# A two-layer transformer block with an expert layer: U runs 26 steps ahead of V, the residual is parked in DRAM, and the gate stage works in two half buffers with chunks of four tokens

## The chip, the cores and the metric

The kernel runs on one core of one Trainium2 chip. The metric is the device time of one execution, in microseconds (us); less is better.

## The reference

512 tokens of width 1024 go through two blocks, in float32. The first adds 16 meta tokens and does grouped-query and differential attention and a gated FFN. The second does latent attention and forgetting attention, and then the PEER expert layer, which this change is about:

```python
qp = (h @ w_pq).reshape(b, s, PEER_HEADS, 2, PEER_HALF)        # 8 heads, 2 halves of 128
sc = jnp.einsum("bshpd,hpnd->bshpn", qp, sub_keys)             # 128 keys in each half
s1, i1 = lax.top_k(sc[..., 0, :], 16);  s2, i2 = lax.top_k(sc[..., 1, :], 16)
cand = (s1[..., :, None] + s2[..., None, :]).reshape(b, s, 8, 256)
top_s, top_c = lax.top_k(cand, 16)
expert = e1 * 128 + e2                                         # e1, e2: the keys that top_c names
gate = jax.nn.softmax(top_s, axis=-1)
y = sum over heads and selected experts of  gate * gelu(u_expert . h) * v_expert
x = x + gate2 * y
```

There are 16384 experts (128 first keys times 128 second keys), each with a row of 1024 in `peer_u` and one in `peer_v`.

## The kernel before

Everything up to the second attention and its output projection (`mixed_linear`) is not touched. The rest has five stages.

**Key scores.** TensorE (`pe`) projects the queries and multiplies them with the keys, 16 pieces; ScalarE (`act`) evacuates them into `sc` (part of the SBUF arena `r2`).

**Sort.** VectorE (`v`) does `key_tops` and `pair_tops` for each of 8 heads and the first three of four token tiles (`DT` = 3, 384 tokens, `DN`); 24 pairs. `top_done` counts them.

**Picks.** `tile_picks(t)` finds, for each tile, the keys of the 128 chosen experts of a token: `pair_ranks`, a one-hot over 16 ranks (`hot`, 2048 elements a partition, L1470), a multiply (L1473) and a reduction (L1475), twice, then the softmax sums. TensorE turns the result around (`slot_transposes`) and ScalarE evacuates it to `slotT`.

**Gates.** For the three tiles the chosen experts are not gathered; all 16384 are computed, and a dense matrix of gates (token by expert) says what counts. For every token it is the product of two one-hot matrices: VectorE writes `one1` for a chunk of eight tokens in one operation (L1531) and `one2` in eight (L1535, one a token, which multiplies the gate in); TensorE does one 128x128 matmul a token (L2056); ScalarE copies 4 tokens at a time from PSUM to `stage` (L901), one buffer for a whole tile, 8 MB. SyncE (`sp`) stores the tile to the DRAM tensor `gd` in four pieces of 2 MB (`store_gates`, L439), and ScalarE may write the next tile only when they have landed (`stage_free`). Two chunk buffers stand in a ring.

**Expert loop.** Step i takes the 128 experts with second key i. The U part (`experts_in`): load 512 KB of `peer_u`, transpose it (`u_transposes`, two halves), split it into a high part (ScalarE, `u_high`, L845) and a rest (VectorE, `u_low`, L1488), three matmuls for each of eight pieces against the split tokens (`hidden`, L2007), and a gelu (ScalarE) into a slot of `act_ring`. The V part (`experts_out`, L2023): multiply the ring slot with the gates (`w_mul`), split that and 512 KB of `peer_v`, and 18 matmuls of 512 columns, which add up in six PSUM banks over all 128 steps. The gates come back 768 KB at a time for four steps (`load_gates`, L447). U runs `AHEAD` = 16 steps ahead of V: two such steps lie before the chunks, twelve among them (one after every fourth chunk), two after, and the loop does the other 112 along with V; its last 16 steps have V alone. The first `u_transposes` stands in TensorE's queue behind all key scores, and VectorE's first `u_low` behind all sorting.

The fourth tile's 128 tokens are done otherwise: GpSimd (`pool`) gathers single rows of U and V by indirect DMA (512 KB for 128 tokens), VectorE does one dot or one multiply-add for each of the 2 x 128, spread evenly over the steps from `FIRST_ROW` = 4 to `LAST_ROW` = 112, and sorts this tile's heads there too.

The residual `x` (2 MB) stays in SBUF to the end, where VectorE adds the expert sums and SyncE stores the result.

Each engine works its queue off in the order of the code and waits on semaphores; SyncE's queue holds all loads and stores of this part in one written-out order.

Of the kernel before, what the change touches and what calls it, by code (L numbers as in the profile page):

```python
# [15 lines left out]
P = 128  # L16
D = 1024
# [21 lines left out]
AHEAD = 16  # L39
CHUNK = 8  # L40
# [3 lines left out]
FIRST_ROW, LAST_ROW = 4, 112  # L44
# [29 lines left out]
def build(nc, wst, wada, x_in, meta_in, cols_in, rowsa_in, rowsb_in, rope_in, const_in, pos_in,  # L74
          subk_in, peer_u, peer_v, out):
    ctx = ExitStack()
    with ctx:
# [149 lines left out]
        keys = cut(r1, 10752, NKEYS)  # L227
# [7 lines left out]
        act_ring = cut(r2, 0, AHEAD, DN)  # L235
# [10 lines left out]
        stage = cut(big, 0, NKEYS, P)  # L246
        one1 = cut(r1, 0, 2, CHUNK, P)
        one2 = cut(r1, 2 * CHUNK * P, 2, CHUNK, P)
        slotT = [gates[:, 0, 0:384], gates[:, 0, 384:768], r1[:, 10240:10624]]
        hot = cut(big, 0, SLOTS, TOPK)  # L250
        ranks = cut(big, 2048, 2, SLOTS)
        rank_bits = cut(big, 2304, 2, SLOTS).bitcast(U32)
        topf = cut(big, 2560, 2, PH, TOPK)
        wrap = cut(big, 2816, SLOTS)
        picks = cut(big, 2944, DT, 2, SLOTS)

        gring = cut(big, 0, 2, DT, GB * P)
# [21 lines left out]
        gd = nc.dram_tensor("gd", (DT, P, NKEYS * P), F32).ap()  # L279
# [42 lines left out]
        one1_ready, one2_ready, g_acc, g_ev = (sem(n) for n in ("one1_ready", "one2_ready", "g_acc", "g_ev"))  # L322
        g_out = [sem(f"g_out{q}") for q in range(4)]
# [11 lines left out]
        y_ready, y_out = sem("y_ready"), sem("y_out")  # L335
# [64 lines left out]
        def stage_free(eng, t):  # L400

            if t:
                for q in range(4):
                    eng.wait_ge(g_out[q], 16 * t)
# [5 lines left out]
        def _(sp):  # L410
# [25 lines left out]
            def store_gates(t):  # L436
                sp.wait_ge(g_ev, 2 * NCH * (t + 1))
                for q in range(4):
                    sp.dma_start(gd[t][:, 4096 * q:4096 * q + 4096], stage[:, 32 * q:32 * q + 32, :].rearrange("p e t -> p (e t)")  # L439
                                 ).then_inc(g_out[q], 16)  # L440

            def load_gates(b):
                if b % 8 == 0:
                    sp.wait_ge(g_out[b // 8], 16 * DT)
                if b >= 2:
                    sp.wait_ge(w_done, GB * (b - 1))
                sp.dma_start(gring[:, b % 2],  # L447
                             gd[:, :, GB * P * b:GB * P * b + GB * P].rearrange("t p n -> p t n")).then_inc(g_in[b % 2], 16)
# [5 lines left out]
            for j in range(9, 12):  # L454
                load_u(j)
            store_gates(1)
            for j in range(12, 16):
                load_u(j)
            store_gates(2)
            sp.wait_ge(g_acc, 2 * DT * NCH)  # L460
            for i in range(VR):
                load_v(i)
            for b in range(2):
                load_gates(b)
            for j in range(AHEAD, AHEAD + 2):
                load_u(j)
            for i in range(NE):
                if i + AHEAD + 2 < NE:
                    load_u(i + AHEAD + 2)
# [5 lines left out]
            sp.dma_start(out[DT], x[:, DT, :]).then_inc(y_out, 16)  # L475
            for t in range(DT):
                sp.wait_ge(y_ready, t + 2)
                sp.dma_start(out[t], x[:, t, :]).then_inc(y_out, 16)
# [4 lines left out]
        def _(pool):  # L483
# [44 lines left out]

            for q in range(2, 4):
                pool.wait_ge(g_out[q], 16 * DT)  # L530
# [11 lines left out]
        def _(act):  # L542
# [298 lines left out]
            def u_high(s):  # L841
# [3 lines left out]
                act.activation(uT_hi[:, s % 2], ps[:, 1, :].rearrange("p (k n) -> p k n", k=KD // 2), ACT.Copy  # L845
# [14 lines left out]
            def gelu(j):  # L860
# [3 lines left out]
                act.activation(act_ring[:, j % AHEAD, :], ps[:, 0, 0:DN], ACT.Gelu_apprx_tanh,  # L864
# [14 lines left out]
            def slots_evac(t):  # L879
                act.wait_ge(slot_tr, t + 1)  # L880
                act.activation(slotT[t], ps[:, 2 + t % 2, 0:384], ACT.Copy).then_inc(slot_ready, 1)

            for s in range(3):
# [1271 lines left out]
```

## Time and profile before

| | |
|---|---|
| median of 3 runs | 2830.1 us (2827.2 to 2830.22) |
| the profiled execution: its time, its span | 2838.91 us, 2837.1 us |
| TensorE matmul busy | 2532.2 us (89%) |
| VectorE busy | 1786.5 us (63%) |
| ScalarE busy | 955.8 us (34%) |
| GpSimd busy | 355.3 us (13%) |
| mean granted TensorE clock | 0.955 |
| moved by DMA | 427.20 MB, mean 151 GB/s |

Times in rows are counted from the start of the span. "Busy" is a share of the whole span, over stages that have different limits, so the stages are read one by one below. The granted clock is a share of 2.4 GHz. PE is TensorE, PEld its weight loads, DVE VectorE, ACT ScalarE, POOL GpSimd, SP SyncE; a q behind a name is the engine's queue. In the program's names `r` stands for the arenas `r1` and `r2`.

### The profile page before, as it was taken

Reading aid. Unit: us, or ns where it says so; the run is one execution under the profiler, and the core shown is the slowest. Engines: PE = TensorE matmul, PEld = TensorE weight load, DVE = VectorE, ACT = ScalarE, POOL = GpSimd, SP = SyncE. Lnnn points to the kernel's source line nnn. Section 1 sums busy time; section 2 is a strip of 40 time slices with the busy share of each in tenths; the row PEclk is TensorE's granted clock in tenths of the full one; section 3 lists DMA queues with packets and bytes.
Section 4 is the critical chain, followed back from the end, with each engine's and each line's share of the span. In section 5 each row is a group of like instructions: output and inputs, shape, how many; then the busy total and the mean of one; then the engine's idle time right before and its main releaser. Section 6 shows DMA issues by size and latency. Waiting matters only on the chain.

```text
span 2837.1 us, 37492 instructions
## 1 busy us (share of the span) xinstructions
PE 2532.2 (89%) x13633; PEld 2153.2 (76%) x13633; DVE 1786.5 (63%) x3871; ACT 955.8 (34%) x1639; POOL 355.3 (13%) x326
## 2 busy tenths in 40 slices
PE   8999888999989969989256669999999999999998
PEld 6777776777779747854156668898989898899986
DVE  5535646553244455458887657877777777776675
ACT  3334412222224446311134444333333333333332
POOL 1001100110000000100000001232222222222220
PEclk9999989999999989999678899999999999999999
DMA  4110005662222110030003345787777777777764
GB/s 172 61 45 1 1 33 183 228 216 88 79 86 75 60 45 1 1 126 1 8 23 141 149 170 190 261 292 261 268 261 270 265 269 267 266 272 277 244 224 141
DMA packets 107908, 427.20 MB, mean 151 GB/s; under 512 B 11328, under 2 KB 11584, under 8 KB 97104
## 3 DMA queue, kind: packets, MB, share of 16 engines
q1 hardware_dynamic: 62624, 262.17, 26.2%
q0 software_dynamic: 44064, 160.98, 16.3%
q8 instruction: 111, 1.82, 0.3%
q10 hardware_dynamic: 1040, 1.67, 0.2%
q14 instruction: 69, 0.57, 0.1%
HBM read 397.51 MB, written 27.26 MB: 150 GB/s over the span
## 4 chain that ended last, share of the span: by engine, by line
PE 73%; DVE 14%; issue 4%; ACT 4%; DMA 2%; DVEq 2%; ACTq 1%; SPq 1%; POOLq 0%
PE ps L2023 16%; PE ps L2007 15%; PE ps L1808 9%; PE ps L1762 7%; PE ps L1678 5%; PE ps L1830 4%; PE ps L1996 3%; PE ps L2056 3%; PE ps L1743 2%; DMA gd<-big 1%; PE ps L1948 1%; PE ps L1715 1%; PE ps L1929 1%; ACT r L639 1%; PE ps L1730 1%
## 5 line engine op out<-in xcount | busy, mean ns | idle before, releaser
L2007 PE MATMUL ps<-hd_hi,uT_hi 128*128 128x384 f32 x1024 | 349.4, 341 | 0.7 <-ACT r L864 0.7
L2007 PE MATMUL ps<-hd_hi,uT_lo 128*128 128x384 f32 x1024 | 347.4, 339 | 0.0
L2007 PE MATMUL ps<-hd_lo,uT_hi 128*128 128x384 f32 x1024 | 347.3, 339 | 0.0
L1488 DVE TENSOR_TENSOR uT_lo<-ps,uT_hi 128x512 fp32r<-128x512 f32 x256 | 176.7, 690 | 255.0 <-ACT uT_hi L845 254.8
L2023 PE MATMUL ps<-v_hi,ew_hi 128*128 128x512 f32 x768 | 320.4, 417 | 3.9 <-DVE v_lo L1493 2.1
L2023 PE MATMUL ps<-v_hi,ew_lo 128*128 128x512 f32 x768 | 303.1, 395 | 0.0
L2023 PE MATMUL ps<-v_lo,ew_hi 128*128 128x512 f32 x768 | 300.9, 392 | 0.0
L537 POOL DMA_INDIRECT big<-peer_u,r x128 | 136.0, 1062 | 861.6 <-DVE r L1563 524.8
L845 ACT ACTIVATE uT_hi<-ps 128x512 fp32r<-128x512 f32 x256 | 152.9, 597 | 266.3 <-PE ps L1996 266.3
L864 ACT ACTIVATE r<-ps,zero 128x384 f32<-128x384 f32 x128 | 74.3, 581 | 472.0 <-PE ps L2007 467.7
L1996 PE MATMUL ps<-const,r 128*128 128x128 f32 x1024 | 155.3, 274 | 52.5 <-DVE uT_lo L1488 32.9
L2007 PEld LDWEIGHTS ps<-hd_hi,uT_hi 128*128 128x128 f32 x1024 | 193.6, 189 | 10.0 <-issue 1.1
L2007 PEld LDWEIGHTS ps<-hd_hi,uT_lo 128*128 128x128 f32 x1024 | 193.3, 189 | 9.7
L2007 PEld LDWEIGHTS ps<-hd_lo,uT_hi 128*128 128x128 f32 x1024 | 193.3, 189 | 0.0
L537 POOL DMA_INDIRECT big<-peer_v,r x128 | 144.4, 1128 | 386.2 <-DVE big L1591 369.8
L1493 DVE TENSOR_TENSOR v_lo<-r,v_hi 128x1024 fp32r<-128x1024 f32 x128 | 156.8, 1225 | 34.3 <-ACT v_hi L852 34.3
L1996 PEld LDWEIGHTS ps<-const,r 128*128 128x128 f32 x1024 | 126.4, 141 | 65.6 <-DVE uT_lo L1488 25.5
L1591 DVE SCALAR_TENSOR_TENSOR big<-big,r 128x1024 f32<-128x1024 f32 x128 | 164.5, 1285 | 16.6 <-DMA big<-peer_v,r 4.3
L2023 PEld LDWEIGHTS ps<-v_hi,ew_lo 128*128 128x128 f32 x768 | 144.2, 188 | 32.6
L2023 PEld LDWEIGHTS ps<-v_hi,ew_hi 128*128 128x128 f32 x768 | 144.7, 188 | 27.9 <-DVE v_lo L1493 4.6
L2023 PEld LDWEIGHTS ps<-v_lo,ew_hi 128*128 128x128 f32 x768 | 145.2, 189 | 24.3
L1073 DVE TENSOR_TENSOR w_lo<-big,w_hi 128x2048 fp32r<-128x2048 f32 x42 | 96.2, 2290 | 106.1 <-ACT w_hi L632 106.1
(332 smaller groups left out, 5335.2 us busy)
## 6 DMA issues: line engine op xcount, KB each, us to landing
big<-wst SPq DMA_DIRECT2D x70, 1024.0 KB, 4.8
r<-peer_u SPq DMA_DIRECT2D x128, 512.0 KB, 7.2
r<-peer_v SPq DMA_DIRECT2D x128, 512.0 KB, 5.2
r<-wada POOLq DMA_DIRECT2D x48, 512.0 KB, 4.7
gd<-big SPq DMA_DIRECT2D x12, 2048.0 KB, 15.1
big<-gd SPq DMA_DIRECT2D x32, 768.0 KB, 9.4
x<-x_in SPq DMA_DIRECT2D x4, 512.0 KB, 6.7
big<-peer_u,r POOLq DMA_INDIRECT x128, 6.4
```

What stands on the lines that cost most here:

```text
L537: pool.indirect_dma_start(rows[n % RW], None, table, bass.IndirectOffsetOnAxis(ap=idx[:, n:n + 1], axis=0)).then_inc(got[n % RW], 16)
L845: act.activation(uT_hi[:, s % 2], ps[:, 1, :].rearrange("p (k n) -> p k n", k=KD // 2), ACT.Copy).then_inc(u_hi_done, 1)
L1488: v.tensor_tensor(uT_lo[:, s % 2], ps[:, 1, :].rearrange("p (k n) -> p k n", k=KD // 2), uT_hi[:, s % 2].bitcast(F32), ALU.subtract).then_ ...
L1493: v.tensor_tensor(v_lo[:, i % VR, :], vraw[:, i % VR, :], v_hi[:, i % 2, :].bitcast(F32), ALU.subtract).then_inc(v_lo_done, 1)
L1591: v.scalar_tensor_tensor(out=yacc[:, n % 2, :], in0=vrows[n % RW], scalar=wts[:, n:n + 1], in1=yacc[:, n % 2, :], op0=ALU.mult, op1=ALU.ad ...
L1678: mm = pe.matmul(ps[0:r, bank, 0:w], hT[:, k, t * P:t * P + r], wt[:, k, 0:w], start=(k == 0), stop=(k == KD - 1))
L1762: mm = pe.matmul(ps[:, bank, 0:256], h[:, k, t * P:(t + 1) * P], w[:, k, :], start=(k == 0 and i == 0), stop=(k == KD - 1 and i == 2))
L1808: mm = pe.matmul(ps[:, 2 * (f % 2) + u, :], w[:, k, u, :], h[:, k, 0:512], start=(k == 0 and i == 0), stop=(k == KD - 1 and i == 2))
L1830: mm = pe.matmul(ps[:, 2 * t + half, :], a[:, f % 2, t * P:(t + 1) * P], w[:, f % 2, 512 * half:512 * half + 512], start=(f == 0 and i == ...
L1996: mm = pe.transpose(ps[:, 1, P * k:P * k + P], uraw[:, j % UR, at:at + P], ident)
L2007: mm = pe.matmul(ps[:, 0, 0:DN], w[:, k, :], h[:, KD // 2 * half + k, :], start=(half == 0 and k == 0 and i == 0), stop=(half == 1 and k = ...
L2023: mm = pe.matmul(ps[:, 2 + 2 * t + half, :], w[:, P * t:P * t + P], vv[:, 512 * half:512 * half + 512], start=(i == 0 and n == 0), stop=(i ...
```

## The change

It does the following.

- `AHEAD` is 26. Nine U steps (0 to 8) are put into the sort and just behind it: from the 17th of the 24 sorts on, VectorE does two `u_low` behind each sort (`hidden_low`), a ninth pair comes after the ranks of tile 0. Steps 9 and 10 follow, twelve come among the chunks (one after every eighth chunk of four), three after the chunks. The loop has 102 U steps, and 26 with V alone.
- Until U is 26 ahead, its transposes use two PSUM banks in turn (`in_bank`), not one.
- The 26 slots of `act_ring` need room: ten lie in the SBUF of `x`. So `x` is stored to a DRAM tensor `xd` before (ScalarE's first `u_high` waits for that), and loaded back into `xback` at step 106, for the end. `LAST_ROW` is 102: the 256 row operations are spread over 98 steps. The last sum of the fourth tile comes at step 112, as before.
- The gates are built in chunks of four tokens, in a ring of four buffers (`one`); one PSUM bank holds a chunk. `stage` is two buffers of half a tile (64 tokens, 4 MB) each. ScalarE issues their stores itself, four of 1 MB, behind the last copy of the half. `gd` has six halves, so a load of gates for four steps has runs of 1 KB, not 2 KB.
- The picks: the one-hots of both keys stand in one buffer. `tile_ranks(t)` writes them, and the multiply is done by GpSimd (`slot_keys`; for tile 0 VectorE does one of the two). `tile_picks(t)` waits for that and does one reduction for both keys. Tile 0 is picked before the chunks; tiles 1 and 2 are picked by VectorE in the middle of the chunks of the tile before (ranks after its third chunk, the rest after its seventh).
- SyncE asks for the U load 26 ahead of the gate loads and keeps three U loads ahead, not two.

```diff
-AHEAD = 16
-CHUNK = 8
+AHEAD = 26
+INX = 10
+FIRST = 11
+EVERY = 8
+HT = P // 2
+CHUNK = 4
-FIRST_ROW, LAST_ROW = 4, 112
+FIRST_ROW, LAST_ROW = 4, NE - AHEAD
...
+        def in_bank(s):
+
+            return 3 if s % 2 and s < 2 * AHEAD else 1
...
             sp.wait_ge(mixt_tr, 2 * T)
-            for j in range(9):
+            for j in range(UR):
                 load_u(j)
-            store_gates(0)
...
+            sp.wait_ge(out_add, 8 * T)
+            for t in range(T):
+                sp.dma_start(xd[t], x[:, t, :]).then_inc(x_out, 16)
+            for j in range(UR, AHEAD):
                 load_u(j)
...
+            load_u(AHEAD)
             for b in range(2):
                 load_gates(b)
...
+                if i == LAST_ROW + 4:
+                    sp.wait_ge(u_row, SLOTS)
+                    sp.wait_ge(v_row, SLOTS)
+                    sp.wait_ge(x_out, 16 * T)
+                    for t in range(T):
+                        sp.dma_start(xback[t], xd[t]).then_inc(x_back, 16)
...
+            def slot_keys(t):
+                pool.wait_ge(ranks_ready, t + 1)
+                for a in range(2 if t else 1):
+                    hk = hot[:, a].rearrange("p (h k) r -> p h k r", h=PH)
+                    mk = pool.tensor_tensor(hk, hk, each_pick(a), ALU.mult)
+                mk.then_inc(hot_ready, 1)
...
+            def hidden_evac(j):
+                u_high(2 * j + 1)
+                u_high(2 * j + 2)
+                gelu(j)
...
+                    if at + CHUNK == HT:
+                        act.wait_ge(g_ev, n + 1)
+                        for q in range(4):
+                            act.dma_start(gd[h][:, 32 * HT * q:32 * HT * q + 32 * HT],
+                                          stage[h % 2][:, 32 * q:32 * q + 32, :].rearrange("p e t -> p (e t)")).then_inc(g_out[h % 2][q], 16)
+                    if n % EVERY == EVERY - 1:
+                        hidden_evac(FIRST + n // EVERY)
...
+            def hidden_low(steps):
+                for j in steps:
+                    u_low(2 * j + 1)
+                    u_low(2 * j + 2)
...
                     pair_tops(t, h).then_inc(top_done, 1)
+                    u = DT * h + t - 16
+                    if u == 0:
+                        u_low(0)
+                    if u >= 0:
+                        hidden_low([u])
+            tile_ranks(0)
+            hidden_low([8])
...
+            tile_picks(0)
+            hidden_low([9])
             for t in range(DT):
                 v.wait_ge(slot_ready, t + 1)
                 for c in range(NCH):
                     n = t * NCH + c
+                    if n == 3:
+                        hidden_low([10])
+                    if n >= 4:
+                        v.wait_ge(g_acc, n - 3)
+                    v.tensor_tensor(one[n % 4][0], each(keys, CHUNK), over(slotT[t][:, CHUNK * c:CHUNK * c + CHUNK], NKEYS),
+                                    ALU.is_equal)
...
+                    if t < DT - 1 and c == 2:
+                        tile_ranks(t + 1)
+                    if t < DT - 1 and c == 6:
+                        tile_picks(t + 1)
```

## Rows read from the trace of the kernel before

**Rows 1.** Busy by stage: span, PE, PEld, DVE, ACT, POOL, PEclk, DMA share, GB/s:

```profile
1360.00:1450.00 90.00, 16.25 (x78) 14.65 (x76) 74.01 (x177) 8.59 (x14) 0.00 (x0) 0.58 0.04 12
...
1449.30:1516.10 66.80, 52.95 (x380) 49.84 (x379) 59.16 (x161) 37.60 (x44) 0.00 (x0) 0.97 0.10 30
1516.10:1537.00 20.90, 5.60 (x43) 5.25 (x41) 10.25 (x28) 0.90 (x2) 0.00 (x0) 0.72 0.96 408
...
1912.90:2755.00 842.10, 836.33 (x4513) 758.32 (x4512) 628.73 (x997) 289.76 (x471) 229.40 (x209) 1.00 0.76 264
2768.10:2826.20 58.10, 58.09 (x251) 47.28 (x252) 30.33 (x39) 19.18 (x26) 0.00 (x0) 1.00 0.44 141
```

**Rows 2.** Chain that ended last, one loop step apart (start, length):

```profile
2679.22 2.77 PE ps L2023 x12
...
2688.47 2.77 PE ps L2023 x12
```

**Rows 3.** Timeline of TensorE, the first transposes of U:

```profile
1359.86 0.60 PE L1996 MATMUL ps<-const,r 128*128 128x128 f32 x4
1385.76 1.11 PE L1996 MATMUL ps<-const,r 128*128 128x128 f32 x4 [25.30 <-DVE uT_lo L1488]
```

**Rows 4.** Timeline of VectorE, end of the sort and a tile's picks:

```profile
1379.31 0.22 DVE L1450 TENSOR_SCALAR r<-r 128x16 f32<-128x16 f32 x1
...
1384.70 0.22 DVE L1450 TENSOR_SCALAR r<-r 128x16 f32<-128x16 f32 x1
...
1391.56 0.28 DVE L1467 CAST big<-r 128x256 f32<-128x256 uint32 x1
...
1393.36 2.29 DVE L1470 TENSOR_TENSOR big<-big,const 128x2048 f32<-128x2048 f32 x1
...
1408.59 0.29 DVE L1467 CAST big<-r 128x256 f32<-128x256 uint32 x1
```

**Rows 5.** VectorE in the gate stage: timeline, then lines (min/median/max, first to last):

```profile
1484.84 1.22 DVE L1531 TENSOR_TENSOR r<-r,gates 128x1024 f32<-128x1024 f32 x1
1485.97 2.14 DVE L1535 TENSOR_SCALAR r<-r,gates 128x128 f32<-128x128 f32 x8
1488.03 1.22 DVE L1531 TENSOR_TENSOR r<-r,gates 128x1024 f32<-128x1024 f32 x1
...
1498.20 0.69 DVE L1488 TENSOR_TENSOR uT_lo<-ps,uT_hi 128x512 fp32r<-128x512 f32 x1 [0.54 <-ACT uT_hi L845]
...
L1531 DVE TENSOR_TENSOR r<-r,gates x32: 1210/1215/1226, 1449.3 to 1586.9; 128x1024 f32<-128x1024 f32 x32
...
L1535 DVE TENSOR_SCALAR r<-r x128: 335/342/348, 1591.2 to 1670.6; 128x128 f32<-128x128 f32 x128
```

**Rows 6.** Waits from 1300 to 1740 (total, times, longest):

```profile
ACT big L901 <- DMA gd<-big: 37.3, 2, 18.7
```

**Rows 7.** Timelines of SyncE and TensorE at the hand-over:

```profile
1674.23 3.07 SPq L439 DMA_DIRECT2D gd<-big  x4
...
1681.24 5.32 SPq L447 DMA_DIRECT2D big<-gd  x2
...
1706.62 1.12 PE L1996 MATMUL ps<-const,r 128*128 128x128 f32 x4 [19.61 <-DMA r<-peer_u]
...
1712.94 0.47 PE L2023 MATMUL ps<-v_hi,ew_hi 128*128 128x512 f32 x1 [1.80 <-DVE ew_lo L1508]
```

**Rows 8.** A load issued by ScalarE (timeline), and SyncE's gate stores (their line):

```profile
2.15 0.62 ACTq L546 DMA_DIRECT2D r<-rope_in x1
...
L439 SPq DMA_DIRECT2D gd<-big x12: 326/671/1371, 1513.9 to 1676.0; - x12
```

**Rows 9.** VectorE's combining line in attention, and GpSimd beside it (timeline):

```profile
L1101 DVE SCALAR_TENSOR_TENSOR r<-r,coef x16: 767/768/2993, 205.1 to 359.6; 128x528 f32<-128x528 f32 x16
...
341.38 2.62 DVE L1101 SCALAR_TENSOR_TENSOR r<-r,coef 128x528 f32<-128x528 f32 x1
...
338.90 4.53 POOL L492 TENSOR_TENSOR w_lo<-big,w_hi 128x2048 fp32r<-128x2048 f32 x1
```

More of the change, by code:

```diff
@@ L244, in build @@
         gst = cut(r2, 16960, 2, T * PH)
-        stage = cut(big, 0, NKEYS, P)
-        one1 = cut(r1, 0, 2, CHUNK, P)
-        one2 = cut(r1, 2 * CHUNK * P, 2, CHUNK, P)
+        stage = [cut(big, NKEYS * HT * b, NKEYS, HT) for b in range(2)]
+        one = [[cut(r1, CHUNK * P * (2 * b + a), CHUNK, P) for a in range(2)] for b in range(4)]
         slotT = [gates[:, 0, 0:384], gates[:, 0, 384:768], r1[:, 10240:10624]]
[L250 to L257, printed above, removed]
+        xback = [cut(big, 8192 + D * i, D) for i in range(T)]
+        hot = cut(r2, 0, 2, SLOTS, TOPK)
+        rank_bits = cut(r2, 14368, 2, SLOTS).bitcast(U32)
+        ranks = cut(r2, 14624, 2, SLOTS)
+        wrap = cut(big, NKEYS * P, SLOTS)
+        topf = cut(r1, 11104, 2, SLOTS)
+        picks = [v.rearrange("p (a s) -> p a s", a=2) for v in (gates[:, 0, 768:1024], r1[:, 10848:11104], rowsb[:, 0:256])]
+        gring = cut(big, 0, 2, 2 * DT, GB * HT)
         w_of = cut(big, 4096, 2, DN)
@@ L434, in load_v @@
                 sp.dma_start(vraw[:, i % VR, :], v_by_key[:, i, :]).then_inc(v_load[i % VR], 16)
[L436 to L440, printed above, removed]
             def load_gates(b):
                 if b % 8 == 0:
-                    sp.wait_ge(g_out[b // 8], 16 * DT)
+                    gates_out(sp, b // 8)
                 if b >= 2:
@@ L908, in _ @@
-            for j in range(2 + 4 * DT, AHEAD):
-                u_high(2 * j + 1)
-                u_high(2 * j + 2)
+            act.wait_ge(x_out, 16 * T)
+            u_high(0)
+            for j in range(9):
+                hidden_evac(j)
+                if j in (5, 6, 7):
+                    gate_exps(j - 5)
+            slots_evac(0)
+            for j in range(9, FIRST):
+                hidden_evac(j)
+            for t in range(DT):
+                for c in range(NCH):
+                    n = t * NCH + c
+                    h, at = n * CHUNK // HT, n * CHUNK % HT
+                    if at == 0:
+                        stage_free(act, h)
+                    act.wait_ge(g_acc, n + 1)
+                    act.activation(stage[h % 2][:, :, at:at + CHUNK].rearrange("p e t -> p t e"),
+                                   ps[:, 4 + n % 4, :].rearrange("p (t e) -> p t e", t=CHUNK), ACT.Copy).then_inc(g_ev, 1)
+                    if t < DT - 1 and c == 16:
+                        slots_evac(t + 1)
+                    if at + CHUNK == HT:
[5 more added lines that the diff above has]
+                        hidden_evac(FIRST + n // EVERY)
@@ L911, in _ @@
+            for j in range(FIRST + DT * NCH // EVERY, AHEAD):
                 if j < AHEAD - 1:
-                    gelu(j)
+                    hidden_evac(j)
+                else:
+                    u_high(2 * j + 1)
+                    u_high(2 * j + 2)
             w_high(0)
@@ L1483, in tile_picks @@
                 v.tensor_tensor(g, g, over(gst[:, 1, PH * t:PH * t + PH], TOPK), ALU.mult)
+                if t == 0:
+                    hk = hot[:, 1].rearrange("p (h k) r -> p h k r", h=PH)
+                    v.tensor_tensor(hk, hk, each_pick(1), ALU.mult)
+                    v.drain()
+                v.wait_ge(hot_ready, t + 1)
+                v.tensor_reduce(picks[t], hot, AX.X, ALU.add)
                 v.drain().then_inc(picks_ready, 1)
@@ L2041, in _ @@
             u_transposes(0)
-            experts_in(0)
-            for t in range(DT):
-                slot_transposes(t)
-            experts_in(1)
+            for j in range(9):
+                experts_in(j)
+            slot_transposes(0)
+            for j in range(9, FIRST):
+                experts_in(j)
             for t in range(DT):
```

181 lines of the change are left out of this document (81 added, 100 removed).

## The prediction

> **What bounds the kernel now.** I read the page's slices first. The reader is to see that PE is full in the last 40% of the span and has its one deep hole just before it; so the question is what fills the hole and what the last part costs per step. Then the stages [rows 1]: in the expert loop (1912.9 to 2755) PE is busy 836.3 of 842.1 us, DVE 75%, DMA 76% at 264 GB/s. That loop is bound by TensorE. One of its steps is 9.25 us [rows 2]. The last steps, without U, are 252 matmuls (14 steps of 18) in 58.1 us [rows 1], 4.15 us each. So a U step (8 transposes, 24 matmuls) costs 9.25 - 4.15 = 5.10 us of PE wherever PE is full, and nothing where PE is idle. From 1360 to 1450 PE is busy 16.3 of 90 us at a granted clock of 0.58, a mean over its two levels of 1.2 and 2.4 GHz [rows 1]: VectorE is sorting and picking.
>
> Next the hole itself. PE does its first U transposes at 1359.86 and then waits 25.3 us for VectorE's first split of U [rows 3]. VectorE sorts until 1384.9, one (tile, head) every 5.39 us, then makes three tiles' picks at 17.03 us each (1391.56 to 1408.59) [rows 4], ending at 1442.6. Of a tile's 17.03 the ranks take 1.8 (to 1393.36), the gate sums about 1.0, and six operations over 2048 elements the rest, 2.37 each with their gaps (2.29 without). In the gate stage VectorE writes a chunk of eight tokens in 3.19 us (1.13 the first one-hot, 2.06 the eight others) and serves one U step per four chunks [rows 5]; the chunk stage is VectorE's, except for two stalls in which ScalarE waits 37.3 us for the single stage buffer to be stored [rows 6]. Last, the hand-over: the last store is issued at 1674.2, the gates are asked for at 1681.2, PE waits 19.6 us for a U load that queued behind all that, and the first V matmul starts at 1712.94 [rows 7].
>
> **Part 1, ten U steps leave the loop.** 112 U steps become 102: 10 x 5.10 = **-51.0 us**, if PE stays the bound. What gets tighter is VectorE: the 256 row operations are now spread over 98 steps and not 108, 2.61 a step for 2.37, so 0.24 x 1.3 us = 0.3 us more in 9.25, from 75% to about 79%. DMA gains 0.24 x 0.5 MB a step, 13 GB/s on 264. Both stay below PE, but heads' sorting steps fall more often on steps with three rows; I charge **+3 us** (bounds 0 and +12).
>
> **Part 2, the sort stage gets nine U steps.** The first split can't come before PE's transposes at 1359.9 and ScalarE's copy, 1361.1. VectorE is through with its seventeenth sort at 1346.9 (1384.7 [rows 4] less seven of 5.39, with the last operation of 0.2) and so stands still for 14 us. This is the cost that the edit hides: the PE queue, where the U work stands behind all key scores. Then u_low 0, 1 and, after one `hidden` (2.1 us) and its transposes, u_low 2: about 1366.2. The other seven sorts now carry two splits each, 5.39 + 2 x 0.65 = 6.7 us (PE needs 5.1 per step, so it keeps up): 1366.2 + 47 = 1413. The picks of tile 0: ranks 1.8 us, two one-hots of 2.37, so 1419.6; two splits, the keys, the gate sums (1.0), one multiply 2.37, a reduction over twice the elements (2 x 2.29 less one overhead, 4.45). With the lock of part 3 this ends at 1431.4. The splits 19 and 20 then wait for PE (slot transposes, one `hidden`), as they did before (6.7 us from 1442.6 to 1449.3); with two banks I take 5.7. Chunks start at **1437**, and did at 1449.3 [rows 5].
>
> **Part 3, the gate stage.** A chunk of four is one one-hot of 128x512 (0.69, the length of u_low [rows 5], less 0.08 overlap = 0.61) and four of 0.2575: 1.64 us; 96 make 157.4. Twelve pairs of splits, 1.3 each: 15.6. The stage buffer is halved and doubled; a half takes over 30 us to fill, a store of 4 MB at 408 GB/s [rows 1] takes 10: the 37.3 us of waiting vanish. Two tiles' picks moved in here: ranks and one-hots 6.5, gates and reduction 5.5: 24.0. The store issues are now on ScalarE: its issues take up to 0.62 us, SyncE's 0.67 in the median [rows 8]. Four, 2 us or more, stand ahead of u_high; the evacuation of the last chunk before it leaves about 0.9 us of slack there, so VectorE waits about 1 us at five halves: +5 (bounds 0 and 12).
> What remains is GpSimd's multiply, 4.53 us for 128x2048 [rows 9]. VectorE's own was 2.37. Is it free, being beside VectorE? The trace speaks against it. A VectorE operation with two SBUF inputs has a median of 768 ns, but 2.62 us where it starts at 341.38 beside a GpSimd multiply that ends at 343.43: it ends 0.57 us after that one. The longest, 2993 ns, lies the same way [rows 9]. So VectorE's two-input work stood still until GpSimd was done. The one-hots have two SBUF inputs; I charge the whole of the four multiplies of tiles 1 and 2, 4 x 4.53 = 18 us, and tile 0 about 2 (in part 2). Bounds: 0 and 22.
> The Trainium skill (SBUF — State Buffer, "Who interferes with whom") says the same: the port pair is locked for a whole instruction by VectorE with two SBUF inputs or in a two-port mode, or by GpSimd, and the other blocks. By it the sum is as here; a reader who takes engines as independent gets 20 us less.
> Sum: 157.4 + 15.6 + 24.0 + 18 + 5 = 220. The last one-hot ends at **1657** (before 1670.9 [rows 5]).
>
> **Part 4, the hand-over.** PE has four U steps left, about 5.2 each: 1657.6 + 21 = 1678.5, then 2 us until the weights are there (1.8 before). The data: from 1659 on 4 MB of gates, 1.5 of V, 0.5 of U, 1.5 of gates back, 7.5 MB at 400 GB/s = 19 us: 1678. The U load no longer stands behind the gate loads. V starts at about **1681**, 32 us before 1712.9. If the small runs of the gate loads (1 KB for 2 KB) land late, this grows by some 5 us; none of this stage is at full rate otherwise.
>
> **Part 5, the residual.** Four stores of 0.5 MB queue on SyncE behind three U loads, which started at 1260; nothing needs them before 1359.9, so 95 us hide about 5. The reload (2 MB) comes at step 106, in the stage that moves 141 GB/s at a DMA share of 0.44 [rows 1]; V loads queue behind it, a step later. 0 to 1 us. The end (11 us of sums and stores after the last matmul at 2826) is as it was.
>
> **Sum** against the profiled execution (span 2837.1, 2838.9 with what lies around): -32 - 51 + 3 = -80, so 2759. The median of the runs is 8.8 us below that execution: **2750**.
>
> **Rivals.**
> A: the two engines do not hinder each other in these forms (the trace has no one-hot beside a GpSimd operation). Then 20 us less, 2730. For it: nothing but that it hasn't been seen.
> B: VectorE is not kept fed in the gate stage: ScalarE's stores, its copies in strides, and the order split, gelu, evacuation in one queue hold up `u_hi_done`, say 1.5 us more at each of 24 splits; 24 x 1.5 = 36, of which GpSimd's blocks already cover some, so about +20 us: 2770. Against: ScalarE has only 37.6 of 66.8 us busy in the stage now [rows 1].
> C: the loop gives back. If the denser rows let VectorE's lateness through, 0.3 us in each of 98 steps, +29: 2778. Against: PE idle in the loop is 5.8 us in all [rows 1].
> D, slower than before: the loads bind the loop. Each step moves 2.5 MB, with denser rows 2.62, and the gates come in runs half as long. It takes 80 us to eat the gain, 0.8 us in each of 102 steps: a step of 10.05 us, a rate of 261 GB/s. The loop sustains 264 now at a share of 0.76 [rows 1], so this needs a fall of the rate itself.
> E: no change: ten U steps saved but the front loses all it wins and 50 more; the PE idle there is too large for that.
>
> **How the numbers follow.** Likeliest as summed 0.45; A 0.18; B 0.19; C 0.13; D 0.03; E 0.02. The range 2722 to 2784 leaves out about 2 in 10 (half of the far ends of A and C, D, E). Measurement tells 0.2%, 6 us, from no change: faster 0.95, same 0.02, slower 0.03.
>
> **What would show it.** In the changed trace: VectorE idle about 14 us before its first split near 1347; sorts at 6.7 us after; chunks from 1437 at 1.64 us, and one-hots of several us wherever GpSimd multiplies (right) or of their usual length (A); no wait of ScalarE for a gate store; last one-hot at 1657; first V matmul at 1681; a loop step of still 9.25 us, 26 last steps of 4.15. The prediction is wrong if the loop step is longer, or if the first V matmul comes after 1700.

## The result: 2793.6 us, 1.4% faster, half of what was forecast

| | before | after |
|---|---|---|
| median, lowest to highest (4 runs each) | 2830.16 us, 2827.2 to 2832.83 | 2793.55 us, 2787.02 to 2798.95 |
| ratio to before, 95% interval | 1 | 0.9859 (0.9841 to 0.9876) |
| the profiled execution: time, span | 2838.91, 2837.1 us | 2790.66, 2788.9 us |
| mean granted TensorE clock | 0.955 | 0.965 |

The forecast was 2750 us with a range of 2722 to 2784. The sign was right, the size was not: 36.6 us came, 80 had been worked out. The page of the kernel after: busy time by engine, then the slices of PE, its granted clock and the DMA share; the last line is PE's in the kernel before.

```profile
PE 2545.9 (91%) x13633; PEld 2162.6 (78%) x13633; DVE 1795.6 (64%) x3911; ACT 965.7 (35%) x1644; POOL 390.0 (14%) x331
...
PE   8999888999989969989857789999999999999998
...
PEclk9999989999999979999989899999999999999999
DMA  4110005662221210021113246787878778787764
...
PE   8999888999989969989256669999999999999998
```

The hole in front of the expert loop is smaller: its lowest slice is 5 tenths, not 2. GpSimd has 390.0 us for 355.3, the five multiplies among them. The stages, as in [rows 1]; first the sort and tile 0's picks, then the gate stage, the hand-over, a piece of the loop and the last steps without U:

```profile
1360.00:1437.00 77.00, 56.14 (x307) 51.19 (x305) 66.56 (x230) 25.11 (x38) 4.50 (x1) 0.93 0.20 69
1437.00:1670.00 233.00, 169.57 (x1134) 161.56 (x1135) 204.34 (x513) 112.72 (x131) 18.89 (x4) 0.88 0.30 116
1670.00:1698.20 28.20, 22.45 (x138) 21.07 (x137) 7.59 (x11) 9.70 (x17) 0.00 (x0) 1.00 0.94 345
1910.00:2640.00 730.00, 719.08 (x3849) 651.14 (x3848) 562.45 (x900) 251.20 (x408) 226.00 (x198) 0.99 0.79 274
2700.00:2777.80 77.80, 75.56 (x323) 61.23 (x322) 42.83 (x54) 25.19 (x34) 0.00 (x0) 0.98 0.46 146
```

Two things differ from what was expected. In the gate stage VectorE is busy only 204.34 of 233 us, although its work sets that stage's length. In the loop PE is idle 10.9 of 730 us and the mean clock is 0.99; before it was 5.8 of 842 at 1.00 [rows 1].

From here on the path is cut at four points that each trace shows: the first one-hot of the chunks, the start of the last one, the first V weight load, and the last V weight load. In front of them stands the last weight load of the query projection (3 us before the last key score; "last query" in the table), up to which only SyncE's part is changed: the stores of `x`. It comes at 1355.5 us in the profile before and at 1347.5 after, at 1344.9 to 1352.1 in the experiments on the changed kernel: profiles of the same code differ by that much. So stages are compared, not times.

| us | last query | to first one-hot | chunks | to first V matmul | V loop |
|---|---|---|---|---|---|
| before | 1355.5 | 93.8 | 221.3 | 42.3 | 1113.1 |
| after | 1347.5 | 84.0 | 237.5 | 29.1 | 1079.5 |
| e1_sync_stores | 1344.9 | 84.0 | 212.9 | 28.2 | 1074.2 |
| e2_act_stores_late | 1346.6 | 84.0 | 213.9 | 28.9 | 1076.4 |
| e3_vector_multiplies | 1348.1 | 84.0 | 233.7 | 29.0 | 1074.1 |
| e4_rows_to_112 | 1350.5 | 86.8 | 234.9 | 29.0 | 1095.9 |
| b1_rows_to_102 | 1349.0 | 94.2 | 219.3 | 42.2 | 1122.1 |
| e5_picks_in_two_steps | 1346.6 | 84.0 | 212.9 | 28.4 | 1062.9 |
| e6_sync_stores_vector_multiplies | 1352.1 | 83.1 | 210.4 | 28.5 | 1079.0 |
| e7_start_late_every_six | 1344.9 | 66.7 | 217.2 | 28.1 | 1074.1 |
| e8_all_four | 1352.0 | 64.4 | 214.5 | 28.4 | 1062.6 |

**Where it went.** The first V matmul was forecast for 1681 us and the V loop at 1113.1 - 51 + 3 = 1065 us; measured are 1698.2 and 1079.5. So the miss of 31.7 us (2790.7 against 2759) is 17.2 in front of the loop and 14.4 in it. In front: chunks began at 1431.6, not 1437 (-5.4: 8.0 earlier on account of the untouched part, 2.6 later by their own), took 237.5, not 220 (+17.5), and the hand-over took 29.1, not 24 (+5.1).

**The gate stage.** Timeline of ScalarE in the kernel after, where the first half of a tile is full:

```profile
1482.50 1.11 ACT L938 ACTIVATE big<-ps 128x512 f32<-128x512 f32 x1 [0.56 <-PE ps L2125]
1483.64 3.73 ACTq L945 DMA_DIRECT2D gd<-big  x4
1487.47 1.08 ACT L875 ACTIVATE uT_hi<-ps 128x512 fp32r<-128x512 f32 x2 [3.86 <-issue]
```

and of VectorE, which waits for that `u_high`, here and three halves later:

```profile
1488.10 0.69 DVE L1542 TENSOR_TENSOR uT_lo<-ps,uT_hi 128x512 fp32r<-128x512 f32 x1 [3.60 <-ACT uT_hi L875]
...
1610.06 0.69 DVE L1542 TENSOR_TENSOR uT_lo<-ps,uT_hi 128x512 fp32r<-128x512 f32 x1 [3.64 <-ACT uT_hi L875]
```

The four issues hold ScalarE for 3.7 us. The prediction had 2 us and 0.9 us of slack. All five halves inside the stage show it; their VectorE waits are 3.60, 3.91, 3.48, 3.64 and 3.51 us, 18.1 in all. Behind three of them comes another, of 1.1 to 2.1 us, for the chunk matmuls that now run late (5.1 in all). The waits of the whole stretch from 1400 to 1700, after; the last line is ScalarE's own:

```profile
DVE uT_lo L1542 <- ACT uT_hi L875: 45.6, 18, 5.6
...
ACT uT_hi L875 <- issue: 19.5, 5, 4.2
...
DVE r L1596 <- PE ps L2125: 5.1, 3, 2.1
```

**The lock.** GpSimd's multiplies in the kernel after (timeline), and what VectorE did beside them:

```profile
1409.38 4.50 POOL L552 TENSOR_TENSOR r<-r 128x2048 f32<-128x2048 f32 x1 [199.62 <-DVEq L1510]
1443.07 9.49 POOL L552 TENSOR_TENSOR r<-r 128x2048 f32<-128x2048 f32 x2 [29.19 <-DVEq L1510]
1530.52 9.40 POOL L552 TENSOR_TENSOR r<-r 128x2048 f32<-128x2048 f32 x2 [77.96 <-DVEq L1510]
```

```profile
1406.97 9.07 DVE L1509 TENSOR_TENSOR r<-r,const 128x2048 f32<-128x2048 f32 x2
...
1444.29 3.89 DVE L1596 TENSOR_TENSOR r<-r,gates 128x512 f32<-128x512 f32 x1
1448.10 5.32 DVE L1600 TENSOR_SCALAR r<-r,gates 128x128 f32<-128x128 f32 x4
1453.34 0.68 DVE L1596 TENSOR_TENSOR r<-r,gates 128x512 f32<-128x512 f32 x1
```

One chunk, 1.6 us a little later, takes 9.1 us here (1444.29 to 1453.4): GpSimd multiplies from 1443.07 to 1452.56. So the forecast's lock holds, in forms that the trace before did not show: the one-hot goes up to 4.42 us from 0.68, and a `tensor_scalar` with one SBUF tensor input (its two scalars come from SBUF too) to 4.55 from 0.34. Four operations in the gate stage are held up so, by 15.3 us in all. Tile 0's two one-hots take 9.07 us for 2 x 2.29: the second is held up by 4.4.

**The loop.** Timelines of VectorE and TensorE in the kernel after, at the step behind the one with the fourth tile's head picks:

```profile
1925.46 1.22 DVE L1650 CUSTOM_DVE_ANT_0 big<-big,r 128x1024 f32<-128x1024 f32 x1
...
1926.60 0.25 DVE L1621 CAST r<-r 128x16 f32<-128x16 uint32 x2
...
1931.39 0.18 DVE L1632 CAST r<-r 128x16 uint32<-128x16 f32 x1
1931.87 0.56 DVE L1557 TENSOR_TENSOR big<-big,r 128x384 f32<-128x384 f32 x1 [0.30 <-issue]
1932.34 0.68 DVE L1542 TENSOR_TENSOR uT_lo<-ps,uT_hi 128x512 fp32r<-128x512 f32 x1
```

```profile
1933.17 0.66 PE L2067 MATMUL ps<-const,r 128*128 128x128 f32 x4 [2.65 <-DVE uT_lo L1542]
...
1934.48 0.63 PE L2094 MATMUL ps<-v_hi,ew_lo 128*128 128x512 f32 x1
1934.91 0.63 PE L2094 MATMUL ps<-v_hi,ew_hi 128*128 128x512 f32 x1
...
1937.28 0.39 PE L2094 MATMUL ps<-v_hi,ew_hi 128*128 128x512 f32 x1
1937.51 0.40 PE L2094 MATMUL ps<-v_lo,ew_hi 128*128 128x512 f32 x1
```

Here VectorE has three row operations (1922.33 to 1926.6) and the picks, 5 us (1926.60 to 1931.6), in one step. `u_low` is late, PE waits 2.65 us, and then the first matmuls of V follow each other every 0.43 us where it is 0.23 otherwise: the granted clock from 1933.7 to 1937.1 is 0.51, the lower of its two levels, which costs eight matmuls 1.6 us. The step is 13.64 us long, 4.39 more than 9.25. Four steps behind picks look like this (13.64, 13.54, 13.32, 13.3), each with 3.4 us at the low clock. In the kernel before the steps behind picks are 10.4 to 11.0 us, and the clock is never low from the first V matmul to the last.

Three rows beside the picks are not enough to explain it. The kernel before has such a step too (VectorE's rows and the first operation of its picks, then TensorE's wait behind them):

```profile
2080.96 1.28 DVE L1591 SCALAR_TENSOR_TENSOR big<-big,r 128x1024 f32<-128x1024 f32 x1
...
2082.77 1.21 DVE L1581 CUSTOM_DVE_ANT_0 big<-big,r 128x1024 f32<-128x1024 f32 x1
...
2084.08 1.28 DVE L1591 SCALAR_TENSOR_TENSOR big<-big,r 128x1024 f32<-128x1024 f32 x1
2085.28 0.24 DVE L1552 CAST r<-r 128x16 f32<-128x16 uint32 x2
...
2091.49 0.63 PE L1996 MATMUL ps<-const,r 128*128 128x128 f32 x4 [1.33 <-DVE uT_lo L1488]
```

What does separate the steps is the number of rows in the three steps that a head takes (two of sorting, then the picks), as `row_step` and `head_step` of the kernel give it. From the third head on it is 7 for all six heads before, with waits of 0.96 to 1.54 us behind the picks. After it is 8 for four heads, whose waits are 2.65, 2.52, 2.52 and 2.28 us, and 7 for the other two, whose waits are 1.36 and 0.96. In the last two of a head's three steps VectorE is busy 8.1 to 8.9 of 9.25 us and hardly ever waits for `u_high` any more (0.2 us, once): what is left of a step is less than the 1.3 us of one row more.

Step by step the loop adds up. The excess over 9.25 us is 24.1 us in nine U steps after (1.5 of it in the very first, at the low clock) and 9.1 in seven before: +15.0. The steps without U have 2.4 us more. Together that is the 17.4 by which 1079.5 is over 1113.1 - 51.

### The profile page after: what moved, and what is told of

Its sections match the earlier page's. It is cut to its first block, busy times and chain, and to the rows that moved or that the text cites. A ratio compares the mean times of both kernels' runs of the same rounds, so it can differ in the third digit from the quotient of the medians.

```text
span 2788.9 us, 37588 instructions
## 1 busy us (share of the span) xinstructions
PE 2545.9 (91%) x13633; PEld 2162.6 (78%) x13633; DVE 1795.6 (64%) x3911; ACT 965.7 (35%) x1644; POOL 390.0 (14%) x331
## 4 chain that ended last, share of the span: by engine, by line
PE 73%; DVE 16%; ACT 4%; issue 3%; DVEq 2%; ACTq 1%; DMA 1%; POOL 0%
PE ps L2094 15%; PE ps L2078 14%; PE ps L1878 9%; PE ps L1832 7%; PE ps L1748 5%; PE ps L1900 4%; PE ps L2038 4%; DVE r L1600 3%; PE ps L2067 3%; DVE r L1596 2%; PE ps L1813 2%; PE ps L2018 1%; DVE uT_lo L1542 1%; PE ps L1785 1%; PE ps L1999 1%
## 5 line engine op out<-in xcount | busy, mean ns | idle before, releaser
L1542 DVE TENSOR_TENSOR uT_lo<-ps,uT_hi 128x512 fp32r<-128x512 f32 x256 | 175.7, 689 | 217.2 <-ACT uT_hi L875 216.6
L567 POOL DMA_INDIRECT big<-peer_u,r x128 | 143.0, 1117 | 487.1 <-DVE r L1650 287.3
L1650 DVE CUSTOM_DVE_ANT_0 big<-big,r 128x1024 f32<-128x1024 f32 x128 | 155.4, 1217 | 3.8 <-DMA big<-peer_u,r 3.8
L1832 PE MATMUL ps<-w_lo,h_hi 128*128 128x256 f32 x544 | 153.9, 283 | 0.0
```

The source lines that it names most:

```text
L567: pool.indirect_dma_start(rows[n % RW], None, table, bass.IndirectOffsetOnAxis(ap=idx[:, n:n + 1], axis=0)).then_inc(got[n % RW], 16)
L1542: v.tensor_tensor(uT_lo[:, s % 2], ps[:, in_bank(s), :].rearrange("p (k n) -> p k n", k=KD // 2), uT_hi[:, s % 2].bitcast(F32), ALU.subtra ...
L1650: v.tensor_tensor_reduce(out=urows[n % RW], in0=urows[n % RW], in1=h2, scale=1.0, scalar=0.0, op0=ALU.mult, op1=ALU.add, accum_out=dots[:, ...
L1832: mm = pe.matmul(ps[:, bank, 0:256], h[:, k, t * P:(t + 1) * P], w[:, k, :], start=(k == 0 and i == 0), stop=(k == KD - 1 and i == 2))
```

## The experiments

Each is the kernel after with one edit, unless said otherwise. The brackets hold the kernel before, run on the same chip.

**e1_sync_stores: who issues the gate stores.** Two theories: (1) four issues on ScalarE stand before `u_high`; (2) it is the lock, or a feed of VectorE in general.

```diff
+            store_after = {14 + 2 * h: h for h in range(2 * DT)}
             for j in range(UR, AHEAD):
                 load_u(j)
+                if j in store_after:
+                    h = store_after[j]
+                    sp.wait_ge(g_ev, HT // CHUNK * (h + 1))
+                    for q in range(4):
+                        sp.dma_start(gd[h]..., stage[h % 2]...).then_inc(g_out[h % 2][q], 16)
...
-                    if at + CHUNK == HT:
-                        act.wait_ge(g_ev, n + 1)
-                        for q in range(4):
-                            act.dma_start(gd[h]..., stage[h % 2]...).then_inc(g_out[h % 2][q], 16)
```

> The changed kernel with one part undone: the six half-stage stores are issued by SyncE again (between its U loads), not by ScalarE. Theory 1 (ScalarE's four store issues, 3.7 us in a row, stand ahead of the copy that VectorE's next split waits for; VectorE then idles 3.5 to 3.9 us and TensorE's late hidden costs 2 us more, five times): 2793 falls by 20 to 25 us, to about 2771, and the splits behind a half wait under 1 us. Rival (the waits come from the order split, gelu, evacuation in ScalarE's queue, whoever stores): no change, 2790 to 2797, and the waits of 3.5 us stay.

Measured: 2762.22 us (2757.1 to 2767.41) [2833.31], ratio 0.9755 (0.9739 to 0.9771); 31 us below the kernel after. The chunks take 212.9 for 237.5 us. Waits of e1 from 1400 to 1700, its `u_low` being L1544:

```profile
DVE uT_lo L1544 <- ACT uT_hi L882: 30.7, 18, 3.8
```

15 of 45.6 us of waiting are gone by that row, and at the halves inside the stage no such wait is left. Theory 1 holds, and in the stage its size too (20 to 25 expected): 24.6 us for five halves, 4.9 each. The waits themselves are 3.5 to 3.9; the rest, 1.3 each on average, is what comes late behind them. Some of that may be the clock: after has three stretches at the low clock, 17 us in all (from 1490, 1575 and 1609), that e1 has not. Of the other 6.7 us of the medians 5.3 are in the V loop, whose code is the same: e1 has two stretches at the low clock in it, the kernel after six. That part is not shown to belong to the stores.

**e2_act_stores_late: engine or place?** The stores stay on ScalarE, behind the two `u_high` and the gelu.

```diff
-                    if at + CHUNK == HT:
...
                     if n % EVERY == EVERY - 1:
                         hidden_evac(FIRST + n // EVERY)
+                    if at + CHUNK == HT:
...
```

> The changed kernel with ScalarE's store issues moved behind the two copies and the gelu of the U step, not ahead of them. Theory 1: the split is served first, the stores then delay only the evacuation of the next chunks, for which there are four banks: the same gain as with SyncE's stores, about 2771 (one look, so within 6 us). Rival: what is gained at the splits is lost again as waits for PSUM banks: 2790 or more.

Measured (one run): 2762.8 us; chunks 213.9, so the wait for banks that the rival expected does not come. The issues still take their time. Timeline of ScalarE in e2:

```profile
1486.68 0.58 ACT L894 ACTIVATE r<-ps,zero 128x384 f32<-128x384 f32 x1 [1.51 <-PE ps L2078]
1486.69 3.15 ACTq L947 DMA_DIRECT2D gd<-big  x4
1489.88 1.05 ACT L938 ACTIVATE big<-ps 128x512 f32<-128x512 f32 x1 [2.62 <-PE ps L2125]
```

3.15 us, with only copies of chunks behind them, for which the ring of four chunk buffers and banks is a cushion. So it is the place in the queue that costs, not the engine.

**e3_vector_multiplies: is GpSimd's multiply worth it?** The five multiplies go back to VectorE.

```diff
-            slot_keys(0)
-            for t in range(1, DT):
-                slot_keys(t)
...
-                if t == 0:
-                    hk = hot[:, 1].rearrange("p (h k) r -> p h k r", h=PH)
...
-                v.wait_ge(hot_ready, t + 1)
+                for a in range(2):
+                    hk = hot[:, a].rearrange("p (h k) r -> p h k r", h=PH)
+                    v.tensor_tensor(hk, hk, each_pick(a), ALU.mult)
```

> The changed kernel with the five 128x2048 multiplies of the picks given back to VectorE (2.29 us each there, 4.5 to 4.7 on GpSimd); everything else as changed. Theory 2 (VectorE stands still while GpSimd multiplies): gone are the blocks, 18.9 us in the gate stage and 4.4 us in the second one-hot of tile 0; added are 5 x 2.37 = 11.9 us; so 11 us faster than the changed kernel, about 2782. Rival (the engines work side by side and the long one-hots have another cause): 12 us slower, about 2805.

Measured: 2786.21 us (2781.93 to 2793.2), ratio 0.9842 (0.9824 to 0.9859); 7 us below the kernel after, whose 0.9859 (0.9841 to 0.9876) overlaps that; 11 were expected. Chunks 233.7 for 237.5. The lines of VectorE from 1430 to 1680 in e3 (busy, mean ns):

```profile
L1596 DVE TENSOR_SCALAR r<-r,gates 128x128 f32<-128x128 f32 x256 | 71.1, 342 | 0.0
L1592 DVE TENSOR_TENSOR r<-r,gates 128x512 f32<-128x512 f32 x64 | 43.9, 685 | 5.2 <-PE ps L2121 4.9
```

With no GpSimd multiply beside them the one-hots have their usual length on average, so the 4.4 us ones come from it: the longest one-hot of the chunks is 0.69 us here. **e6_sync_stores_vector_multiplies** is both edits:

> The changed kernel with SyncE's stores and with the five multiplies on VectorE. If the two costs are independent (theory 2 holds beside theory 1): 2762 less the 7 to 11 us that the multiplies gave alone: 2751 to 2755. If part of the blocks is hidden in waits that the stores left: 2758 or more.

Measured: 2758.76 us (2754.2 to 2765.99), ratio 0.9733 (0.9717 to 0.9749), against e1's 0.9755 (0.9739 to 0.9771): the intervals overlap, and 2751 to 2755 had been expected if the two costs were independent. Chunks 210.4 for 212.9. The four multiplies in the stage save VectorE 4 x 2.29 us of its own work, 9.2, and cost by the two pairs 9.2 + 2.5 to 9.2 + 3.8, about 12 to 13 us. VectorE stood still for 15.3 us; the difference comes back as waits, which within the stage rise from 2.2 us in e1 to 6.1 in e6. What the lock takes is a little more in the stage than what the hand-over to GpSimd gives, and the medians show no gain from it either way.

**e4_rows_to_112 and b1_rows_to_102: the denser rows.** e4 undoes the one line in the kernel after, b1 makes it alone in the kernel before. The line does more than its name says: the steps of the heads' sorting and picks are worked out from the rows' (`head_step`), so picks come every 12 or 13 steps, not every 13 or 14, and the fourth tile's last sum and the reload of `x` move along.

```diff
-FIRST_ROW, LAST_ROW = 4, NE - AHEAD
+FIRST_ROW, LAST_ROW = 4, 112
```

> The changed kernel with the row operations of the fourth tile spread to step 112 again (108 steps, 2.37 a step) and not to 102; the reload of the residual comes ten steps later. Theory 3 (denser rows on top of a head's sorting make VectorE late, TensorE waits and its clock drops: single steps of 13.5 us): the steps behind a head's picks fall from 13.5 to about 10.7 us, 12 to 14 us in all; but ten steps that have V alone now carry 2.4 rows each, 5.4 us of VectorE for 4.15 of TensorE, +12 us: in sum 2786 to 2796, and the step lengths tell. Rival (the 13.5 us come from the distance of 26 or from the gate loads' short runs): they stay, and the sum is 2805.

> The kernel before with one constant changed: its 256 row operations end at step 102, not 112, so 2.61 a step for 2.37; U still runs 16 steps ahead, chunks, buffers and stores as before. Theory 3 (the density of the rows at a head's picks makes the long steps, not the distance of 26): the steps behind the picks of a head rise from 10.4 to 11.0 to 12 to 13.7 us, with short drops of the clock there, so the loop grows by 10 to 18 us: 2842 to 2850. Rival (the long steps belong to the new distance, ring or gate loads): 2830 to 2834.

Measured, e4: 2810.09 us (2805.0 to 2814.82), ratio 0.9918 (0.99 to 0.9935), 17 us above the kernel after. Its steps behind the picks are 10.43 to 11.17 us, as before the change, with no low clock among its U steps but the very first: that part was right. But ten steps without U, 103 to 112, now have row operations, and they take 69.1 us for 42.5; 12 more had been expected, 26.6 came, with four stretches at the low clock, 17 us, among them. Waits of e4 from 2650 to 2790:

```profile
PEld ps L2094 <- DVE v_lo L1547: 28.1, 12, 5.3
PE ps L2094 <- DVE v_lo L1547: 22.9, 11, 4.9
```

A step of 4.15 us has no room for 2.4 rows of 1.3 us beside VectorE's own work; a step of 9.25 has. So `LAST_ROW` = 102 is the better of the two in this kernel.

Measured, b1: 2839.56 us (2832.07 to 2845.77, 10 runs) [2833.1, 13 runs], ratio 1.0021 (1.0009 to 1.0033), +6.5 us; its V loop is 9.0 longer. Steps of 11.77, 13.55, 13.28 and 13.65 us appear behind the picks, and three stretches of 3.4 us at the low clock, none of which the kernel before has. Waits of TensorE in the loop of b1 (from 1730), of the kernel after and of e5, below (from 1700); in the kernel before they are 7.6 us in 7 times, 1.5 at most:

```profile
PE ps L1996 <- DVE uT_lo L1488: 14.3, 8, 2.6
```

```profile
PE ps L2067 <- DVE uT_lo L1542: 14.8, 8, 2.6
```

```profile
PE ps L2074 <- DVE uT_lo L1544: 4.5, 7, 0.8
```

So one line, with nothing else of the change, brings the wait of 2.6 us and the low clock behind it; what it changes at the picks is the 8 rows for 7. The size was expected higher, 10 to 18.

**e5_picks_in_two_steps: thin the heaviest step.** This is e1 in which the picks of a head (from the second on) are spread over two steps, one key side in each.

```diff
-            def picks3(h):
+            def picks3(h, sides):
...
+                    elif part == 2:
+                        picks3(h, [0] if h else [0, 1])
+                    elif h:
+                        picks3(h, [1])
```

> The changed kernel with SyncE's stores (2762) and, for heads 1 to 7 of the fourth tile, the picks divided over two loop steps, one key's half in each. Theory 3 (it is the amount of VectorE work in one step, three rows and a part of a head's sorting, that makes TensorE wait and its clock drop): the seven long steps (10.3 to 13.7 us) come down towards 9.25, 8 to 14 us in all: about 2752. Rival (they have another cause, such as the loads): same as 2762, steps of 12 to 13.6 us remain.

Measured: 2746.89 us (2745.7 to 2754.2) [2832.5], ratio 0.9702 (0.9684 to 0.972), 15 us below e1 (the profiled V loop: 11.3); 8 to 14 had been expected. The V loop is 1062.9 us; PE's waits for `u_low` are down to 4.5 us, 0.8 at most, in the row above, no U step but the first (10.8, at the low clock) is over 10.3, and no other U step is at the low clock. All the work is still there; only its crowding into one step is gone.

**e7_start_late_every_six: the 14 us in which VectorE waits.** Timeline of VectorE in the kernel after, its first split:

```profile
1353.21 1.29 DVE L1542 TENSOR_TENSOR uT_lo<-ps,uT_hi 128x512 fp32r<-128x512 f32 x2 [14.35 <-ACT uT_hi L875]
```

VectorE stands still here for the key scores; so e7 is e1 with the splits beginning behind the 21st sort, five U steps in the sort stage and one among the chunks after every sixth chunk.

```diff
-FIRST = 11
-EVERY = 8
+FIRST = 7
+EVERY = 6
...
-                    u = DT * h + t - 16
+                    u = DT * h + t - 20
```

> The changed kernel with SyncE's stores and the U steps shifted: the first split stands behind the 21st sort, not the 17th, five steps (not nine) come before the picks of tile 0, and the twelve among the chunks become sixteen, one after every sixth chunk. Theory 4 (VectorE's 14.4 and 2.9 us of waiting behind the 17th sort are lost time, since TensorE's first transposes stand behind the key scores, and TensorE has room among the chunks): both waits vanish, no work is added: 15 to 17 us faster than 2762, about 2746. Rival (a group of six chunks and a U step is bound by ScalarE, six evacuations and a U step's copies and gelu, 11.7 us, or TensorE's order, not by VectorE's 11.1): half of it is lost, 2754 or more.

Measured: 2754.53 us (2743.91 to 2756.18), ratio 0.9725 (0.9709 to 0.9741), against e1's 0.9755 (0.9739 to 0.9771). By the table the way to the first one-hot is 17.3 us shorter and the chunks are 4.3 longer; from the last query to the first V matmul it is 312.0 us for 325.1, 13.1 less. 7.7 of them show in the medians. About 2746 had been expected, 2754 or more by the rival. The profiled execution, 2743.91, is e7's fastest by 9 us, so how much of the 15 is lost is not settled.

**e8_all_four: the four edits together** (stores on SyncE, multiplies on VectorE, picks in two steps, the late start).

> SyncE's stores, multiplies on VectorE, picks of a head in two steps, and the shifted U steps together. If the four mechanisms are independent: 2762 - 8 - 10 - 16, about 2728. If they cover each other (a wait removed shows the next one behind it): 2740 or more.

Measured: 2730.33 us (2726.56 to 2734.82), ratio 0.9633 (0.9617 to 0.9649), 63 us below the kernel after, near the 2728 expected if the four are independent. It is the best version found. Slices of PE and of its clock in e8:

```profile
PE   8998978999998978989868799999999999999998
...
PEclk9999989999999998999989999999999999999999
```

## Why the prediction was wrong, step by step

**Part 1, ten U steps leave the loop: the -51 us right, the +3 mis-sized.** e5, in which nothing else disturbs the loop, has 1062.9 us against 1113.1: -50.2. The +3 us, for which the bounds were 0 and 12, measured 17.4: 13.5 in the U steps behind the first, which go with the denser rows, 1.5 in the first, 2.4 in the steps without U. b1 has 11.4 in its U steps for the rows alone (and gets 2.5 back at the end of the loop, so +9.0). The prediction looked at the mean load (79% of VectorE) and at PE's idle time of 5.8 us; what counted was the heaviest stretch: a head's three steps with 8 rows, picks at the end. [Rows 1] can't show that; the steps behind the picks in the kernel before, 10.4 to 11.0 us with a PE wait of up to 1.5, could: they were already the place where VectorE is late, and the prediction looked at a regular step only [rows 2]. Rival C's mechanism is this, in four steps of about 13.5 us and not in 0.3 us everywhere. b1, e4 and e5 show the cause, too much VectorE work close together: `LAST_ROW` alone brings it, `LAST_ROW` back removes it from the U steps, picks halved remove it too. That it is the count of 8 for 7 is read from the code and the traces; no run changed the rows of one head alone. The low clock behind each such wait adds 1.6 us; the prediction had no term for it. In e1, whose loop has the same code, two of the four steps are without it and are 11.98 and 11.75 us long for 13.3. The regular step is 9.25 us as forecast, so the sign "a longer loop step" would have pointed to these four alone.

**Part 2, the sort stage: right.** VectorE waits 14.35 us (14 forecast). Behind it the sort with its splits ends at 1405.2, 57.7 us after the last query; 1413 was forecast, 57.5 after its own. Tile 0's picks took 26.4, not 24: the second one-hot was held up by GpSimd's multiply, 4.4 us where "about 2" were charged. That is the 2.6 us by which the chunks began late.

**Part 3, the gate stage: the store term failed.** The step "VectorE waits about 1 us at five halves: +5 (bounds 0 and 12)" measured 24.6 us by e1: 19.6 too little, where the whole stage came out 17.5 above its 220. The issue was priced by a single load of 0.62 us and a median of 0.67, four of them as "2 us or more"; four gate stores in a row take 3.6 to 4.05 us at the five halves. [Rows 7] had a batch of four on SyncE, at 3.07 us. And the slack of 0.9 us, taken from the order of the work before, was not there: the trace shows the split waiting for nearly all of it, and chunk matmuls behind. That is a part of rival B's mechanism: B spread 36 us over 24 splits, and without the stores (e1) no split in the stage waits 0.9 us; that its net 20 us are about the size of the miss is luck. e2 narrows it to the place of the issues. The 37.3 us of ScalarE's waiting for the stage buffer are gone, as forecast. The rest was right too: e1's 212.9 us against 215, the 220 without the stores. In that sum the lock was 18 us; VectorE stood still for 15.3, of which 12 to 13 remain on balance (e1 against e6, after against e3). The Trainium skill (DMA: Bandwidth & Descriptors, "Issuing engines are not separate DMA queues") says that issuing from several engines saves only the sequencer's time for the issue, "usually small relative to the DMA itself". The trace agrees as to size, 3.7 us of issuing for stores that land in 10.0. What it cost here came from the queue that the 3.7 us stood in.

**The lock of the ports: right, rival A refuted.** The one-hots reach 4.42 us. The Trainium skill (SBUF — State Buffer, "Who interferes with whom") also names `tensor_scalar` among the forms that can take the shared pair, which the prediction did not use; 4.55 us for one of 0.34 agrees, though no trace shows in which mode it ran.

**Part 4, the hand-over: 29.1 us, not 24.** The last four stores, ahead of the U step in ScalarE's queue, make VectorE's first split wait 5.6 us and with it TensorE 2.2 us. In e1 TensorE has no such wait, but one of 1.2 for a U load that SyncE now issues behind the stores, and the hand-over is 28.2. And four U steps take 5.65 us each there, not 5.2, since gelu, split and transposes of one step follow each other with nothing else to do (first transposes at 1681.12, 1686.79 and 1692.45). The data were in time; the gates and V loads made nobody wait. The gate loads with their shorter runs land no later: their line on the page is the same before and after. The DMA issues of the kernel after (KB each, us to landing):

```profile
gd<-big ACTq DMA_DIRECT2D x24, 1024.0 KB, 10.0
big<-gd SPq DMA_DIRECT2D x32, 768.0 KB, 9.4
```

**Part 5, the residual: right.** Nobody waits for the stores. Behind the reload a V load comes late, which makes step 109 0.7 us longer (4.81 for 4.15), within the 0 to 1 us. Waits of the kernel after from 1690:

```profile
ACT v_hi L882 <- DMA r<-peer_v: 1.1, 1, 1.1
```

The range failed because the upper bounds of two terms were too near: 12 us each, for 17.4 and 24.6. One was priced from a single issue and the other from a mean load, in places where the batch and the heaviest steps count. Of the two signs of being wrong, the first V matmul at 1698.2 stayed just below its 1700.

**What stays open.** Why the medians move by other amounts than the profiled stages do (e7: 13.1 and 7.7; b1: 9.0 and 6.5; e5's loop: 11.3 and 15), and where the 8.0 us of the untouched part come from: profiles differ in a few stretches at the low clock there, and none of the runs was made to tell them apart.

## What to carry to other kernels

Ask where in an engine's queue a DMA issue stands, and count all of a batch (four took 3.7 us) against the slack of exactly the instruction behind them. Where one engine is full and another at 75 to 80%, read the longest step and what stands in it and in the steps just before it, not the mean: 8 rows for 7 around a head's picks made a wait of 2.3 to 2.65 us out of one of 1.0 to 1.5, and thinning the heaviest step was worth 15 us here with no work removed. Work given to GpSimd while VectorE is on the path must not be paid for with the port that they share: beside multiplies of 4.5 to 5.0 us VectorE's one-hots stood still, and nothing was left of the gain.

## What the runs showed of the hardware that was not expected

- The clock falls within the loop, but not each time. Around waits of TensorE of 2.3 to 2.9 us, with full work on both sides, the granted clock is at the lower level (1.2 GHz) for 3.4 us in some cases: the same four waits have it four times in the kernel after, three times in b1 and e6, twice in e1 and e2, once in e3 and e7, 16 of 28. Behind the first U step none of the waits of up to 2.0 us for a split has it. The same wait can so cost about 2.6 us or 4.3.
- A batch of DMA issues costs more than its median times its number. In the five batches of four gate stores on ScalarE the first two issues take 0.33 to 0.57 us each and the last two 1.25 to 1.79, 3.6 to 4.05 in all; the median of all 24 is 0.6. SyncE's batches of e1 take 3.07 to 4.12.
- A VectorE `tensor_scalar` with one SBUF tensor input stood still beside GpSimd's multiply (4554 ns for 339), as did the two-input one-hot.
